# State recurrence and mixing of an mLSTM/Fourier layer: two blocks made one, and a TensorE loop given a fixed place

## The reference

```python
p = rmsnorm_modulated(x) @ w_in + b_in          # q, k, v, o, gates (4 heads of 128), fourier part u (512)
# mLSTM, forward and backward, in chunks of 128 tokens, per head:
C_loc = einsum("l,lv,lk->vk", w, v, k)           # a chunk's matrix state (and n_loc)
C_new = a * C + b * C_loc                        # recurrence over chunks
h = (S @ v + w_inter * (C @ q)) / den            # intra part and inter part
hm = normalise(h_f + h_b) * head_g * sigmoid(o)
# Fourier: real part of the DFT over (rows, columns, channels of a group), orthonormal
fu = fftn(u, axes=(rows, cols, channels)).real
x = x + gate1 * (concat(hm, fu) @ w_out)
h = rmsnorm_modulated(x)
# expert choice: 16 experts each take 128 latent and 16 context tokens by router affinity, top_k
y = sum_e gate * (silu(h_e @ w1) * (h_e @ w3)) @ w2
out = final_rmsnorm(x + gate2 * y)               # also new_C, new_n, new_m of the context
```

## Time and profile before

| | us |
|---|---|
| median of 3 runs (lowest, highest) | 2356.2 (2355.2, 2358.44) |
| the profiled execution's own time | 2357.64 |
| its span | 2355.8 |
| TensorE busy, share of the span | 2190.1, 93% |
| VectorE, ScalarE, GpSimd busy | 490.4, 358.3, 271.0 |

### The profile page before, as it was taken

How to read it: one execution, slowest core, us unless ns; L and a number is a source line. 1 busy time by engine, 2 the same in 40 slices (tenths; PEclk the granted TensorE clock), 3 DMA queues, 4 the chain that set the end, 5 groups by cost and what they waited for, 6 DMA issues and landing times. The chain is left out here.

```text
span 2355.8 us, 37038 instructions
## 1 busy us (share of the span) xinstructions
PE 2190.1 (93%) x15013; PEld 1892.5 (80%) x15013; DVE 490.4 (21%) x1246; ACT 358.3 (15%) x1012; POOL 271.0 (12%) x266
## 2 busy tenths in 40 slices
PE   7999999859985399999999999999999999999992
PEld 2445554846553399999999999999999999999992
DVE  1111115167774410101011101010111011101102
ACT  1011112313321011101111111011111110111102
POOL 0000000011120102022021020120210201202102
PEclk9999999989998699999999999999999999999996
DMA  9720101163422677697797976977979869779775
GB/s 377 294 99 31 62 31 45 72 241 132 137 91 102 205 251 239 245 363 219 277 325 225 345 245 244 363 218 272 330 224 341 250 243 363 218 268 335 224 255 179
DMA packets 351601, 528.76 MB, mean 224 GB/s; under 512 B 12996, under 2 KB 292284, under 8 KB 348232
## 3 DMA queue, kind: packets, MB, share of 16 engines
q1 hardware_dynamic: 336456, 509.35, 62.4%
q0 software_dynamic: 15104, 18.88, 3.9%
HBM read 492.23 MB, written 35.95 MB: 224 GB/s over the span
## 5 line engine op out<-in xcount | busy, mean ns | idle before, releaser
L1626 PE MATMUL ps_ab<-xeT,ring 128*128 128x144 f32 x8192 | 1009.2, 286 | 14.7 <-DVE xeT L1671 14.7
L1626 PEld LDWEIGHTS ps_ab<-xeT,ring 128*128 128x128 f32 x8192 | 1007.5, 190 | 14.8 <-issue 14.8
L1639 PE MATMUL ps_yy<-hidT,ring 128*128 128x144 f32 x4096 | 504.4, 286 | 0.0
L1639 PEld LDWEIGHTS ps_yy<-hidT,ring 128*128 128x128 f32 x4096 | 502.8, 190 | 0.0
L463 PE MATMUL ps_p<-w_in_sb,hT 128*128 128x512 f32 x720 | 318.1, 595 | 3.0 <-DMA w_in_sb<-in_w_in 3.0
L1675 DVE TENSOR_TENSOR hidT<-silu,ps_ab 128x144 f32<-128x144 f32 x256 | 77.8, 304 | 887.0 <-ACT silu L1593 824.7
L463 PEld LDWEIGHTS ps_p<-w_in_sb,hT 128*128 128x128 f32 x720 | 134.6, 191 | 156.6 <-issue 155.5
L1572 POOL DMA_INDIRECT stream<-ye,slot_row x64 | 101.0, 1578 | 1216.5 <-DVE ye_p L1686 1201.9
L1593 ACT ACTIVATE silu<-ps_ab 128x144 f32<-128x144 f32 x256 | 74.5, 291 | 909.8 <-PE ps_ab L1626 884.4
L1215 PE MATMUL b_z<-y,mixT 128*128 128x512 f32 x288 | 129.7, 604 | 10.3 <-ACT aff L1149 10.3
L1679 DVE STREAM_TRANSPOSE yS<-yT 128x1024 f32<-128x1024 f32 x16 | 19.9, 1245 | 457.3 <-ACT yT_p L1600 457.3
(11 more groups left out here) (250 smaller groups left out, 1082.3 us busy)
## 6 DMA issues: line engine op xcount, KB each, us to landing
ring<-in_exp_w SPq DMA_DIRECT2D x384, 1024.0 KB, 12.3
y<-in_ada_w SPq DMA_DIRECT2D x22, 1024.0 KB, 8.1
w_in_sb<-in_w_in SPq DMA_DIRECT2D x4, 2048.0 KB, 21.5
kv<-kvo SPq DMA_DIRECT2D x15, 512.0 KB, 5.7
kvo<-pr SPq DMA_DIRECT2D x9, 768.0 KB, 3.3
qkT_dram<-qkT SPq DMA_DIRECT2D x9, 512.0 KB, 4.8
qk<-qkT_dram SPq DMA_DIRECT2D x9, 512.0 KB, 5.1
m_in<-m_lanes SPq DMA_DIRECT2D x9, 512.0 KB, 5.8
```

Source lines behind the costliest of these rows:

```text
L1626: mm = nc.tensor.matmul(ps_ab[f % 2][:, N * w:N * w + N], unit[:, k, bass.ts(c, P)], xeT[:, k], start=(k == 0), stop=(k == DT - 1))
L1639: mm = nc.tensor.matmul(ps_yy[d % 2][:, 0:N], unit[:, f % 2, bass.ts(d, P)], hT[:, f], start=(f == 0), stop=(f == FT - 1))
```

## The change

The function `recurrence` is gone; its work is part of `mixing`'s block. TensorE now does, per state step n, the state sums, then `fourier(n+1)`: a pair of two transform units (`z_sum` of 512 columns, and `f_sum` of the pair before). Of 16 pairs, 0 to 8 go with the state steps, 9 to 12 into turn 0 and 13 to 15 into turn 1, with the prompt's transform. The end states are turned after steps 1 and 3. The state sums use one set of banks, with a wait per bank. k and v have 3 slots, which lie in the space of `x_in`, `mixT`, `x2`. SyncE issues mixing's first loads behind the first three kv loads, and the quarters of `w_out` as `g.y` is read. The head gains are applied in ScalarE's copy to `mixT` (four copies in place of one). GpSimd's copy of the Fourier half is moved from turn i to turn i+1. TensorE's loop over the experts starts at slot 0 of a fetch block (256 instructions).

```diff
-def recurrence(nc, g):
-                for n in range(33):                      # TensorE
-                    if n < 32:
-                        z_sum(n)
-                    if n >= 1:
-                        f_sum(n - 1)
...
-                for n in range(TILES - 1):
-                    pe.wait_ge(wv_fwd, n + 1)
-                    pe.wait_ge(wv_bwd, n + 1)
-                    if n >= 2:
-                        pe.wait_ge(state_kept, LANES * (n - 1))
...
 # mixing, SyncE
+                sp.dma_start(c_init[:], ...); sp.dma_start(n_init[:], ...)
+                for n in range(KV):
+                    load_kv(n)
                 load(0, 0, True)
                 load(1, 1, True)
...
+                for n in range(KV, TILES - 1):
+                    load_kv(n)
+                sp.wait_ge(end_kept, 3)
+                (stores of new_C, new_n)
+                sp.wait_ge(kv_summed, TILES - 1)
                 load_x(0, 0)
                 load_x(1, 1)
                 for n in range(DT // 2):
+                    sp.wait_ge(z_summed, (n + 1) * PAIRS // 4)
                     sp.dma_start(g.w_out_sb[:, 2 * n:2 * n + 2], ...)
 # mixing, GpSimd, behind the small operations on ss
-                    if on(i, 0):
-                        if not below(i, 2):
-                            pool.wait_ge(out_summed, 2 * i - 2)
-                        nc.gpsimd.tensor_copy(mixT[:, par, HEADS:DT], g.fuT[:, :, bass.ts(i, P)]).then_inc(mix_pool, 1)
+                    if on(i, 1):
+                        if below(i, 2):
+                            pool.wait_ge(f_kept, PAIRS // 2 + 1)
+                            pool.wait_ge(kv_summed, TILES - 1)
+                        elif not below(i, 3):
+                            pool.wait_ge(out_summed, 2 * i - 4)
+                        nc.gpsimd.tensor_copy(mixT[:, 1 - par, HEADS:DT], g.fuT[:, :, bass.ts(i - 1, P)]).then_inc(mix_pool, 1)
 # mixing, ScalarE
-                        did(nc.scalar.activation(mixT[:, 1 - par, 0:HEADS], b_m[:]..., ACT.Copy), mix_act)
+                        for h in range(HEADS):
+                            did(nc.scalar.activation(mixT[:, 1 - par, h], b_m[:, bass.ts(h, P)], ACT.Copy, scale=head_g[:, h:h + 1]),
+                                mix_act if h == HEADS - 1 else None)
+                for p in range(9):
+                    fourier(p)          # keep_z(p), and keep_f of every second pair
+                    (keep_end(0), keep_end(1) at p == 2, keep_end(2) at p == 4)
 # mixing, ScalarE's turn
+                    fill = (9, 10, 11, 12) if below(i, 1) else (13, 14, 15) if below(i, 2) else ()
                     weigh(i, 0)
+                    fourier(fill[0:1])
                     inter(i, 0)
+                    fourier(fill[1:2])
                     weigh(i, 1)
+                    fourier(fill[2:3]); in turn 1 also keep_f(7), keep_prompt()
                     inter(i, 1)
+                    fourier(fill[3:4])
 # mixing, TensorE
+                def state_sum(n):
+                    pe.wait_ge(wv_fwd, n + 1)
+                    pe.wait_ge(wv_bwd, n + 1)
+                    for r in range(LANES):
+                        bank, at = lane_bank(r)
+                        if n and at == 0:
+                            pe.wait_ge(state_kept, LANES * (n - 1) + min(r + 3, LANES))
+                        mm = nc.tensor.matmul(bank[:, at:at + VW], kv[...], wv[:, n % 2, r], start=True, stop=True)
+                for n in range(TILES - 1):
+                    state_sum(n)
+                    fourier(n + 1)
+                    (turn_end(0), turn_end(1) at n == 1, turn_end(2) at n == 3)
 # TensorE's turn: score, inter(0), fill[0], intra-side work as before with fill[1] ahead of intra(0),
 # fill[2] behind it (in turn 1 then f_sum(15), prompt_sum), inter(1), fill[3], intra(1)
 # experts, TensorE
-                with pe.Fori(0, E) as e:
+                with nc.Fori(0, E, engines=[pe.engine], head_slot={pe.engine: 0}) as e:
```

More of the change, by code:

```diff
@@ L954, in mixing @@
 def mixing(nc, g):
+    KV, PAIRS = 3, 16
     ctx = ExitStack()
@@ L1151, in turn @@
                         inter(i, 0)
+                    for p in fill[1:2]:
+                        fourier(p)
                     if on(i, 2):
@@ L1155, in turn @@
                         weigh(i, 1)
+                        for p in fill[2:3]:
+                            fourier(p)
+                        if fill == (13, 14, 15):
+                            keep_f(PAIRS // 2 - 1)
+                            keep_prompt()
                         inter(i, 1)
-                    if below(i, 2) and not below(i, 1):
-                        scale_out()
+                    for p in fill[3:4]:
+                        fourier(p)
                     if on(i, 3):
@@ L1179, in _, with z_sum, f_sum @@
             def _(pe):
+                def z_sum(p):
+                    if p >= 2:
+                        pe.wait_ge(z_kept, p - 1)
+                    for u in range(2):
+                        grp, kcb = divmod(2 * p + u, 8)
+                        for c, basis in ((0, g.dft_chan_r), (1, g.dft_chan_i)):
+                            mm = nc.tensor.matmul(b_z[p % 2][:, bass.ts(u, 256)], g.y[:, grp, c, bass.ts(kcb, P)], basis,
+                                                  start=(c == 0), stop=(c == 1))
+                    mm.then_inc(z_summed, 1)
+                def f_sum(p):
+                    pe.wait_ge(z_kept, p + 1)
+                    if p >= 2 and p % 2 == 0:
+                        pe.wait_ge(f_kept, p // 2)
+                    for u in range(2):
+                        for c, basis in ((0, g.dft_row_c), (1, g.dft_row_s)):
+                            mm = nc.tensor.matmul(b_m[:, bass.ts(2 * (p % 2) + u, P)], z_sb[:, p % 2, bass.ts(2 * u + c, P)], basis,
+                                                  start=(c == 0), stop=(c == 1))
+                    mm.then_inc(f_summed, 1)
                 def score(i, par, half):
-                    pe.wait_ge(qk_loaded[par], KV_END + 16 * (half + 1))
+                    pe.wait_ge(qk_loaded[par], FRONT_END + 16 * (half + 1))
                     if not below(i, 1):
@@ L1242, in turn @@
                         inter(i, par, 0)
+                    for p in fill[0:1]:
+                        fourier(p)
                     if on(i, 4):
```

356 lines of the change are left out of this document (172 added, 184 removed).

## The result

The changed kernel took 2328.4 us (median of 4 runs, 2327.7 to 2330.4), the kernel before 2357.3 in the runs beside it (4, 2355.2 to 2359.8): ratio 0.988, 95% interval 0.987 to 0.989. That is inside the forecast, 2328 (2319 to 2338). The profiled execution took 2327.72 (span 2325.9), against 2357.64 before: 29.9 us less, where the sum gave 28.6. Two of the terms in it were wrong by about 3 us each, in opposite senses, and the edit that was costed at nothing turned out to carry more than all the others.

A forecast was written before the change was run, and what follows sets the result against it. TensorE bounds the expert loop and the transforms; state steps wait for VectorE, first turns for loads and VectorE's output. Gain 35.7 minus 7.1 given back is 28.6 us, so 2328 us (2323 to 2333 at 0.62; two in ten outside 2319 to 2338).

The forecast's parts named there:

- State loop: Recurrence steps with transform pairs: 4.45 us a step, eight steps 35.6 us, from about 428.9 to 465.5 with end transposes.
- rival B: State steps run in series, 5.64 us each, 9.5 us more in all: 2337 us; chance 0.15.
- Turn 0: First mixing turn, with four transform pairs as fill: 4.5 + 10.5 = 15.0 us, ending at 480.5.
- Turn 1: Second mixing turn: transforms wait on ScalarE's copies, 3 to 4 us in all; first projection starts at 502.7.
- SyncE's order: Loads of w_out's fourth quarter and turn 2 wait until pair 15 is read (490.5): costed at nothing.
- rival C: Loads of w_out or turn 2 land late, up to 4 us more: 2331.5 us; chance 0.06.
- Given back: Mixing turns 3 to 10: later GpSimd copy and ScalarE's four copies cost 7.1 us, bounds 0 and 11.7.
- Turn 3: Mixing turn whose projection waits for the mixT copy, from 557.04 to 559.2: 2.15 us given back.
- Turns 4 to 9: Mixing turns whose router wait absorbs the 1.3 us lag; 0.55 us each given back, 3.3 in all.
- Turn 10: Mixing turn where GpSimd's chain and copy end at 721.1 against 719.43: 1.7 us given back.
- The expert loop's place: TensorE's expert loop with its head at slot 0 still fits in instruction memory: costs nothing, 94.08 us an expert.
- Rival D: Expert loop no longer stays in instruction memory; 3 us a back edge, +45 us: 2373 us; chance 0.05.

The follow-up runs named there:

- before_late_copy: Kernel before the change, with only GpSimd's copy of the spectrum moved a turn later, behind the sum of squares: median 2358.1 us against 2358.0, ratio 1.0004.
- after: The changed kernel itself, against the kernel before: median 2328.4 us, ratio 0.988; profiled execution 2327.72 us.
- act_order: Changed kernel with ScalarE's evictions in turn 1 reordered, ahead of its inter-sum and weighing work: 2324.2 us, median of 2 runs 2323.7.
- copy_gap: Changed kernel with GpSimd's spectrum copy right behind its pow, but held until VectorE's last weighting of the turn: 2323.6 us (median of 2 runs).
- plain_loop: Changed kernel with TensorE's expert loop as before the change, not set on a fetch block: 2503.1 us.
- slot_239: Changed kernel with TensorE's expert loop begun at instruction 239 of a fetch block instead of 0: 2503.7 us.
- copy_early: Changed kernel with GpSimd's spectrum copy right behind its pow, ahead of the sum of squares: 2327.7 us (median of 2 runs).
- best2: Changed kernel with copy_gap's and act_order's edits, and the head-gain and router loads behind the kv loads: median of 5 runs 2318.8 us.
- slot_128: Changed kernel with TensorE's expert loop begun at instruction 128 of a fetch block instead of 0: 2329.4 us.

## Why the prediction was right, point by point

- **The bound, and the place of the gain**: right. The two halves of the interleaving are 15.7 and 11.8 us.
- **State loop**: step 4.45, measured 4.41; one set of banks didn't put the steps in series (rival B). The start (428.9 / 428.47) held. The forecast end was 2.05 us too early: the sum had no clock term and took the kv loads at nothing ("a step is also longer; nothing"), where one of them cost 0.85 us.
- **Turn 0**: 15.0, measured 14.96.
- **Turn 1**: order and waits right, 3.41 us of them. Missing was what such a wait does to the passes behind it: 3.11 us for 1.9. The turn as a whole agrees to 0.6 us, so the other terms were 0.6 too long together (and 490.9 + 1.15 + 1.2 is 493.3, not the 493.7 in the working). Gain to the first projection 33.1, forecast 35.7.
- **SyncE's order**: the last of w_out was asked for at 492.7 and nothing waited on it (rival C no).
- **Given back**: 3.7 for 7.1, and this is the step of the forecast that failed. Turn 3: +2.19 (forecast 2.15). Turns 4 to 9: +2.86 (3.3), but not as 0.55 each: turn 4 has +1.32, as it too has no wait for the router's exponential ahead of it to absorb the lag (564.80 in the kernel before), and turns 5 to 9 have 0.31 in the mean, near the lower bound of 0.33. The period of 24.2 that I named never came; it was 23.6 to 23.9. Turn 10: -1.32, forecast +1.7. The wait that I priced is there, 1.65 at 690.06, but I let it stand alone. The kernel before had a wait of 2.01 at 705.13 and 1.70 of half clock behind it, which the changed kernel, reaching that point with the lag in hand, doesn't have (0.70 and 7.13 us); before_late_copy shows the same with the late copy alone (21.84 for 23.55). Both could be read beforehand: the second projection of turn 9 stood in the trace with 8.83 us beside its neighbours' 7.13.
- **ScalarE's four copies and GpSimd's later copy** are 2.5 and 1.3 us; the sum had both as one chain: its 0.55 in each of eight turns stands for ScalarE, 4.4 of the 7.1, and the other 2.7 for GpSimd's place. Both came out at about half. Of ScalarE's 0.54 us, 0.2 to 0.3 reached the period in turns 5 to 9.
- **VectorE and GpSimd**: that one holds the other was right, and the runs price it: a 0.6 us copy of GpSimd's beside a 0.69 us multiply costs VectorE 0.32, and all of that reaches the turn's period.
- **The expert loop's place**: 94.08 us, cost nothing, against the kernel before. But the reason given, that it fits as it did, hid what the edit is for. The changed code ahead of the loop had moved its natural head from within some 4 instructions of a block's start to about 235, where the body lies in eight blocks. Rival D's mechanism is real; its price was too low (3 us an edge; 7.2 to 11.7 measured), and the pinned head is what kept it off. The page "Runtime: NRT & Kernel Launch" of the Trainium skill, section "Instruction fetch mechanics", says that TensorE's memory holds 2048 instructions, eight blocks, and that a taken branch whose target is outside the current two pages stalls. The traces agree on the stall (4.4 to 5.3 us) and not on the two pages: a loop of seven blocks shows none in 15 back edges.
- The half microsecond left over lies in the first pass over the experts' code (97.1 us before, 96.5 after). Runs of the same code differ there by as much, so it is no effect of the change.

The forecast of 2328 was met because 2.6 us too much gain, 3.4 too much give-back and this 0.5 nearly cancel. The place and the size of the gain were understood; that the total is met to about 1 us is luck.

## What to carry to other kernels

When a change adds or removes code ahead of a long loop, ask where the loop's head falls now, and count the blocks of 256 instructions that its body touches: here seven stay and eight cost 175 us, and the instruction queue's packets per pass show it at once. A wait of TensorE can cost half-clock passes behind it and needs a range for them, and a wait that a change adds may take the place of one further down that had cost more. A small GpSimd operation belongs where VectorE waits anyway; placed "as early as possible" it held VectorE's chain and gave back what it had won.

## What the runs showed of the hardware

- A loop body of eight blocks of TensorE's code did not stay, and all of it was fetched again, 9 packets a pass (14 for 13 blocks: one more than the blocks in both). Seven blocks stayed for 16 passes; no packet came after the first.
- The half clock can return after short waits in the turns: 3.41 us of waits in two pieces (after, turn 1) gave 3.11 us for 16 passes whose full-clock time is 1.95 (act_order, after a wait of 1.15). In copy_gap the same two waits were followed by a row transform at 1.16 us where after has 1.67, and by 1.95 for the prompt. A wait of 2.04 us ahead of turn 3's projection was followed by 7.11 us in after, and by 8.80 in plain_loop and slot_239; waits of 2.01 to 2.30 in turn 9 by 8.83 in the kernel before, copy_early, copy_gap and best2, while copy_early's 1.99 to 2.07 in turns 5 to 8 had 7.13. From the state loop's end to P(2) it took 36.1 us in copy_gap, 37.7 in after and 39.0 in slot_128, where TensorE's instructions are the same; 33.6 in both act_order and best2, whose wait is 1.15. Why the clock falls in one run and not in another stays open.
- VectorE's delay goes to whichever of its small operations meets GpSimd's multiplication: 1.71 us on one, or 0.21 and 1.67 on two, for the same sum within 0.3.
